# Norms between dense phases: the last feature tile and the first scaled tile in halves of 256 tokens, and the last but one tile's squares added on GpSimd

## What is computed

```python
def rms_norm(t, eps=NORM_EPS):
    tf = t.astype(jnp.float32)
    return (tf * lax.rsqrt(jnp.mean(tf * tf, axis=-1, keepdims=True) + eps)).astype(t.dtype)
...
        h = modulate(rms_norm(x), sh1, sc1)
        x = x + 0.5 * g1[:, None, :] * swiglu(h, w_ff1_in[l], w_ff1_out[l])
        h = modulate(rms_norm(x), sh2, sc2)
        z = h @ w_in[l]
...
        x = x + g2[:, None, :] * mixed
        h = modulate(rms_norm(x), sh3, sc3)
        x = x + 0.5 * g3[:, None, :] * swiglu(h, w_ff2_in[l], w_ff2_out[l])
```

## Time and profile before

| | us |
|---|---|
| median of 3 runs | 3761.18 |
| lowest and highest of them | 3758.82, 3763.38 |
| the profiled execution's own time | 3753.36 |
| its span, first to last instruction | 3751.6 |
| TensorE busy in that span | 3540.1 |
| VectorE, ScalarE, GpSimd busy | 1805.4, 1199.0, 626.3 |
| mean granted TensorE clock | 0.98 |

### The profile page before, as it was taken

One profiled execution on the slowest core, in us unless ns is written; L12 is line 12 of the kernel. 1 busy time (PEld: TensorE's weight loads), 2 busy tenths in 40 slices (PEclk: granted clock), 3 DMA queues, 4 the chain that ended last, 5 costly groups with the idle time before them and its releaser, 6 DMA issues. The chain is left out here.

```text
span 3751.6 us, 52300 instructions
## 1 busy us (share of the span) xinstructions
PE 3540.1 (94%) x22236; PEld 2797.3 (75%) x22236; DVE 1805.4 (48%) x2534; ACT 1199.0 (32%) x1659; POOL 626.3 (17%) x428
## 2 busy tenths in 40 slices
PE   7999998988999999999899899999799999989999
PEld 6888773686888788877458688867578887767887
DVE  5666536745544466653574533334543334354332
ACT  3222234523222322233352322233532223343223
POOL 4202002220202020210213020200011210001112
PEclk9999999999999999999999999999999999999999
DMA  6565421002443355532100233222123222122231
GB/s 193 172 200 162 130 69 34 7 26 80 135 152 110 121 160 179 161 126 72 34 7 13 93 90 107 81 74 79 46 79 101 94 87 93 46 68 85 95 101 57
DMA packets 445212, 358.01 MB, mean 95 GB/s; under 512 B 15990, under 2 KB 441012, under 8 KB 444980
## 3 DMA queue, kind: packets, MB, share of 16 engines
q1 hardware_dynamic: 444980, 354.67, 30.1%
HBM read 350.43 MB, written 2.10 MB: 94 GB/s over the span
## 5 line engine op out<-in xcount | busy, mean ns | idle before, releaser
L570 DVE TENSOR_TENSOR ring_wlo<-ring_raw,ring_whi 128x2048 fp32r<-128x2048 f32 (+4 forms) x270 | 576.6, 2136 | 407.6 <-ACT ring_whi L551 375.2
L551 ACT ACTIVATE ring_whi<-ring_raw 128x2048 fp32r<-128x2048 f32 (+3 forms) x278 | 491.1, 1767 | 533.6 <-PE f_ps L860 255.6
L858 PE MATMUL f_ps<-act_hi,ring_whi 128*128 128x512 f32 x1280 | 502.5, 393 | 3.3 <-DVEq L989 3.3
L860 PE MATMUL f_ps<-act_hi,ring_wlo 128*128 128x512 f32 x1280 | 498.6, 390 | 0.0
L859 PE MATMUL f_ps<-act_lo,ring_whi 128*128 128x512 f32 x1280 | 498.1, 389 | 0.0
L948 POOL TENSOR_TENSOR f_glo<-f_v,f_ghi 128x512 fp32r<-128x512 f32 x88 | 237.4, 2698 | 1082.2 <-ACT f_ghi L940 1082.2
L858 PEld LDWEIGHTS f_ps<-act_hi,ring_whi 128*128 128x128 f32 x1280 | 240.4, 188 | 53.8 <-DVEq L989 5.0
L933 ACT ACTIVATE f_t<-f_ps 128x512 f32<-128x512 f32 x88 | 52.6, 598 | 709.2 <-PE f_ps L860 656.3
L860 PEld LDWEIGHTS f_ps<-act_hi,ring_wlo 128*128 128x128 f32 x1280 | 240.2, 188 | 51.2
L858 PE MATMUL f_ps<-f_ghi,ring_whi 128*128 128x512 f32 x704 | 277.4, 394 | 0.0
L859 PEld LDWEIGHTS f_ps<-act_lo,ring_whi 128*128 128x128 f32 x1280 | 240.4, 188 | 48.9
(11 more groups left out here) (515 smaller groups left out, 6110.1 us busy)
## 6 DMA issues: line engine op xcount, KB each, us to landing
ring_raw<-in_w_ff_in SPq DMA_DIRECT2D x176, 512.0 KB, 4.8
f_ada_raw<-in_w_ada SPq DMA_DIRECT2D x128, 512.0 KB, 5.5
ring_raw<-in_w_mlp SPq DMA_DIRECT2D x64, 1024.0 KB, 5.2
ring_raw<-in_w_in SPq DMA_DIRECT2D x42, 1024.0 KB, 5.1
ring_raw<-in_w_ff_out SPq DMA_DIRECT2D x32, 768.0 KB, 4.8
ring_raw<-in_w_ff_out SPq DMA_DIRECT2D x32, 640.0 KB, 4.2
ring_raw<-in_w_out SPq DMA_DIRECT2D x16, 1024.0 KB, 5.2
ada_raw<-in_w_ada SPq DMA_DIRECT2D x16, 512.0 KB, 7.5
```

The costliest lines, as they stand in the source:

```text
L551: eng.activation(self.w_hi[:, i % self.SPLIT, 0:s.nk, 0:w], self.raw[:, i % self.RAW, 0:s.nk, 0:w], ACT.Copy)\
L570: eng.tensor_tensor(self.w_lo[:, i % self.SPLIT, 0:s.nk, 0:w], self.raw[:, i % self.RAW, 0:s.nk, 0:w], self.w_hi[:, i % self.SPLIT, 0:s.nk ...
L858: eng.matmul(out, wh, o_hi[:, a, :], start=(s.first and q == 0), stop=False)
L860: mm = eng.matmul(out, wl, o_hi[:, a, :], start=False, stop=(s.last and q == s.nk - 1))
```

## The change

The last slot before a norm makes its first output tile whole before its second, and signals that (`first_done`). VectorE updates x tile 6 on this signal, and tile 7 in two halves of 256 tokens. GpSimd adds tile 6's squares as well. ScalarE squares tile 7 in halves. TensorE sums each half of the tokens in a bank of its own (the second is one of the phase's own banks), four passes for the sum of GpSimd and four for tile 7, each of 256 columns. ScalarE takes Ln and Exp of the first half, then of the second. In `Norm`, tile 0 is scaled, rounded and subtracted in halves, and VectorE finishes its low part before it scales tiles 1 and 2. The diff, cut to its core:

```diff
+HALVES = (slice(0, S // 2), slice(S // 2, S))
...
 class Norm:
...
+    def steps(self, t):
+
+        return [(HALVES[0], 1), (HALVES[1], 2)] if t == 0 else [(slice(0, S), t + 2)]
+
     def scale(self, eng, t):
-        eng.scalar_tensor_tensor(out=self.part(t), in0=self.k.x[:, t, :], scalar=self.gain[:, t:t + 1], in1=self.k.rstd,
-                                 op0=ALU.mult, op1=ALU.mult).then_inc(self.scaled, 1)
+        for c, n in self.steps(t):
+            eng.scalar_tensor_tensor(out=self.part(t)[:, c], in0=self.k.x[:, t, c], scalar=self.gain[:, t:t + 1],
+                                     in1=self.k.rstd[:, c], op0=ALU.mult, op1=ALU.mult).then_inc(self.scaled, 1)
...
 class Sums:
...
+    def store(self, eng, wait_group, g, s, update):
+
+        if s.index < DT - 2:
+            wait_group(eng, g)
+            for m in (s.index, s.index + 1):
+                update(m, slice(0, S)).then_inc(self.x_done, 1)
+            eng.wait_ge(self.x_done, s.index + 2)
+        else:
+            eng.wait_ge(self.first_done, 1)
+            update(s.index, slice(0, S)).then_inc(self.x_done, 1)
+            wait_group(eng, g)
+            for c in HALVES:
+                update(s.index + 1, c).then_inc(self.x_done, 1)
+            eng.wait_ge(self.x_done, s.index + 3)
 
     def square(self, eng, t):
-        eng.wait_ge(self.x_done, t + 1)
         if t >= 2:
             eng.wait_ge(self.added, max(1, t - 2))
-        eng.activation(self.sq[t % 2], self.k.x[:, t, :], ACT.Square).then_inc(self.squared, 1)
+        for i, c in enumerate(HALVES if t == DT - 1 else [slice(0, S)]):
+            eng.wait_ge(self.x_done, t + 1 + i)
+            eng.activation(self.sq[t % 2][:, c], self.k.x[:, t, c], ACT.Square).then_inc(self.squared, 1)
 
     def add(self, eng, t):
-        if t == 0 or t >= DT - 2:
+        if t == 0 or t == DT - 1:
             return
...
-    def sum(self, eng):
-        eng.wait_ge(self.added, DT - 3)
-        eng.matmul(self.ps[:, :], self.k.ones, self.acc, start=True, stop=False)
-        for t in (DT - 2, DT - 1):
-            eng.wait_ge(self.squared, t + 1)
-            mm = eng.matmul(self.ps[:, :], self.k.ones, self.sq[t % 2], start=False, stop=(t == DT - 1))
-        mm.then_inc(self.summed, 1)
+    def sum(self, eng, banks_free, other_free):
+        eng.wait_ge(self.added, DT - 2)
+        eng.wait_ge(banks_free, other_free)
+        for c, ps in zip(HALVES, self.ps):
+            eng.matmul(ps[:, c], self.k.ones, self.acc[:, c], start=True, stop=False)
+        for i, (c, ps) in enumerate(zip(HALVES, self.ps)):
+            eng.wait_ge(self.squared, DT + i)
+            eng.matmul(ps[:, c], self.k.ones, self.sq[1][:, c], start=False, stop=True).then_inc(self.summed, 1)
 
     def invert(self, eng):
-        eng.wait_ge(self.summed, 1)
-        eng.activation(self.k.rstd, self.ps[:, :], ACT.Ln, scale=1.0 / D, bias=self.k.eps[:, 0:1]).then_inc(self.logged, 1)
-        eng.wait_ge(self.logged, 1)
-        eng.activation(self.k.rstd, self.k.rstd, ACT.Exp, scale=-0.5)
+        for i, (c, ps) in enumerate(zip(HALVES, self.ps)):
+            eng.wait_ge(self.summed, i + 1)
+            eng.activation(self.k.rstd[:, c], ps[:, c], ACT.Ln, scale=1.0 / D, bias=self.k.eps[:, 0:1]).then_inc(self.logged, 1)
+            eng.wait_ge(self.logged, i + 1)
+            eng.activation(self.k.rstd[:, c], self.k.rstd[:, c], ACT.Exp, scale=-0.5)
...
                 norm.scale(eng, 0)
+                norm.take_lo(eng, 0)
                 norm.scale(eng, 1)
-                for t in range(DT):
+                norm.scale(eng, 2)
+                for t in range(1, DT):
                     if t + 2 < DT:
                         norm.scale(eng, t + 2)
                     norm.take_lo(eng, t)
...
                 for q in range(DT):
-                    eng.wait_ge(norm.lo_ready, q + 1)
+                    eng.wait_ge(norm.lo_ready, q + 2)
...
+                if sums and i == n - 1:
+                    for q in range(s.nk):
+                        mm = block_of(q, 0)
+                    mm.then_inc(sums.first_done, 1)
+                    for q in range(s.nk):
+                        mm = block_of(q, 1)
```

More of the change, by code:

```diff
@@ L590, in round_hi @@
     def round_hi(self, eng, t):
[L591 to L607 removed]
+        for c, n in self.steps(t):
+            eng.wait_ge(self.scaled, n)
+            if self.shift is None:
+                ins = eng.activation(self.hi[:, t, c], self.part(t)[:, c], ACT.Copy)
+            else:
+                ins = eng.activation(self.hi[:, t, c], self.part(t)[:, c], ACT.Identity, bias=self.shift[:, t:t + 1])
+            ins.then_inc(self.hi_ready, 1)
@@ new lines, in take_lo @@
+    def take_lo(self, eng, t):
+        for c, n in self.steps(t):
+            eng.wait_ge(self.scaled, n)
+            eng.wait_ge(self.hi_ready, n)
+            part, hi = self.part(t)[:, c], self.hi[:, t, c].bitcast(F32)
+            if self.shift is None:
+                ins = eng.tensor_tensor(self.lo[:, t, c], part, hi, ALU.subtract)
+            else:
+                ins = eng.scalar_tensor_tensor(out=self.lo[:, t, c], in0=part, scalar=self.shift[:, t:t + 1], in1=hi,
+                                               op0=ALU.add, op1=ALU.subtract)
+            ins.then_inc(self.lo_ready, 1)
@@ L710, in products @@
         if sums:
-            sums = Sums(nc, k, ctx, name, rest, *room)
+            sums = Sums(nc, k, ctx, name, rest, ps[len(groups) % 2][0], *room)
         n_pairs = side.pairs if side else 0
@@ L849, in _, with block_of @@
                 o_hi, o_lo = operands[s.rhs]
-                for q in range(s.nk):
-                    a = s.k0 + q
-                    need(eng, own, base, s, q)
-                    if kind is Plain and g == 0:
-                        eng.wait_ge(norm.lo_ready, a + 1)
-                    for b, (c, w) in enumerate(s.tiles):
-                        out = ps[g % 2][b][0:w, :]
-                        wh, wl = ring.w_hi[:, at, q, c:c + w], ring.w_lo[:, at, q, c:c + w]
-                        eng.matmul(out, wh, o_hi[:, a, :], start=(s.first and q == 0), stop=False)
-                        eng.matmul(out, wh, o_lo[:, a, :], start=False, stop=False)
-                        mm = eng.matmul(out, wl, o_hi[:, a, :], start=False, stop=(s.last and q == s.nk - 1))
+                def block_of(q, b):
+                    c, w = s.tiles[b]
+                    a, out = s.k0 + q, ps[g % 2][b][0:w, :]
+                    wh, wl = ring.w_hi[:, at, q, c:c + w], ring.w_lo[:, at, q, c:c + w]
+                    eng.matmul(out, wh, o_hi[:, a, :], start=(s.first and q == 0), stop=False)
+                    eng.matmul(out, wh, o_lo[:, a, :], start=False, stop=False)
+                    return eng.matmul(out, wl, o_hi[:, a, :], start=False, stop=(s.last and q == s.nk - 1))
+                if sums and i == n - 1:
[4 more added lines that the diff above has]
+                        mm = block_of(q, 1)
+                else:
+                    for q in range(s.nk):
+                        need(eng, own, base, s, q)
+                        if kind is Plain and g == 0:
+                            eng.wait_ge(norm.lo_ready, s.k0 + q + 1)
+                        for b in range(len(s.tiles)):
+                            mm = block_of(q, b)
                 mm.then_inc(ring.slot_done, 1)
@@ L866, in _ @@
             if sums:
-                sums.sum(eng)
+                sums.sum(eng, banks_free, len(groups) - 1)
 def weights(w, l, col, width, k0, nk):
```

62 lines of the change are left out of this document (19 added, 43 removed).

## The result

| | before | after |
|---|---|---|
| median, us (lowest to highest, executions) | 3760.0 (3753.63 to 3763.38, 4) | 3732.21 (3730.37 to 3737.76, 4) |
| after over before | 1 | 0.9929 [0.9913, 0.9945] |
| the profiled execution, us | 3753.36 | 3732.57 |
| its span, us | 3751.6 | 3730.9 |

The changed kernel is faster by 0.71%. Its median lies 9.6 us under the forecast of 3741.8 and 2.8 us under the low end of the range.

What follows compares the result with a forecast made beforehand. TensorE bounds the kernel, waiting on a handover chain at 10 norm places. Gains of 9.35, 6.12, 1.21 + 1.20 and 0.66 + 0.84 sum to 19.4 us off 3761.18: 3741.8 us, 8-in-10 range 3735 to 3749.

Steps and rivals of the forecast that it cites:

- Bounds and places: TensorE bounds the kernel, and waits at 10 places where a dense phase's updated x needs its RMS norm: 8.06 or 7.93 us.
- Tile 6 leaves the chain: Before each norm: tile 6 is complete 4.1 or 5.5 us early; GpSimd's add costs nothing, slack 1.2 to 1.9 us.
- the two new waits: VectorE waits for the last slot's first half, TensorE for the second bank; both cost nothing.
- Halves: Halves cost more than half; sum of squares to rstd gains 1.21 or 1.20 us, rstd to restart 0.66 or 0.84.
- The first phases' 0.66 and 0.84: First f1 and first in2 gain only the rstd-to-restart part: 0.66 and 0.84 us.
- Tile 1 next: After the restart tile 1 comes 2.7 us after low 0, while TensorE has 12 passes on tile 0; no stall booked.
- Clock: Half clock after restarts, cold stretches of 3.2 to 5.7 us: no gain or loss booked, about 2 us of scatter.
- rival 3: GpSimd's tile 6 add is late in part, taking up to 3.33 us: gain 15, time 3746; 7%.
- Halves that don't pay (3765): Each half costs as much as its whole; places lose 0.3 to 0.5 us, no measurable change; 5%.
- The clock that stays up (3720): A restart 1.9 us sooner finds TensorE's clock still up; if no place went cold, 22 us saved; 5%.
- A late tile 6 (3746): GpSimd's tile 6 add ends 2.0 us later, past the slack in four places by 0.9 us; 7%.
- its slower form (3772): The late add stands before all eight passes in TensorE's queue, 3 us a place, slower than before; 3%.

Runs made afterwards that it cites:

- sums part alone: Kernel before with only tile 6 early and added on GpSimd, and tile 7's squares, sums, Ln and Exp in halves; norm unchanged: 3747.22 us, 0.9976 of before.
- tile 0 whole: Changed kernel with the norm's tile 0 whole again, its low part still ahead of scaling tiles 1 and 2: 3741.86 us, 0.9959 of before.

## Why the prediction was wrong, point by point

**Bounds and places: right.** The time went where the ten places are; the rest of the dense stages needs as many matmuls as before. The statement that a length change of the dense stages would speak against the prediction was fair too: the five dense stretches are 2.6 us shorter in sum, which is the half clock behind their restarts.

**Tile 6 leaves the chain: right.** The add was forecast to end at 437.8 in the kernel's old times and ended 1.01 us before the last dense matmul did (438.00, 439.01); forecast was 0.97 (438.77 - 437.8). GpSimd's add took 1283 to 1306 ns in all its 60 instances, as this one group shows:

```profile
L674 POOL TENSOR_TENSOR f_u<-f_u,f_v x20: 1285/1294/1299, 409.7 to 2491.6; 128x512 f32<-128x512 f32 x20
```

None took the 2.3 to 3.3 us of the slower operation in the earlier trace rows. Handing tile 6 back to TensorE costs 7.1 us. Reordered matmuls and the two new waits cost nothing that the timeline shows.

**Halves: right, the sizes within 0.2 us a place.** From the last matmul's end, forecast and measured:

| step | forecast | measured |
|---|---|---|
| sums of the first half begin | 1.03 | 1.08 |
| first Ln | 1.78 | 1.82 |
| first Exp | 2.29 | 2.32 |
| second Ln | 2.74 | 2.65 |
| second Exp ends | 3.67 | 3.56 |
| first scale | 3.96 | 3.84 |
| restart, with shift | 6.19 | 6.01 |
| restart, without shift | 5.89 | 5.79 |

The one term that was too large is ScalarE's: I put the second Ln behind the first Exp's end with 0.03 between, while it began 0.09 ahead of it (441.66, and 441.33 + 0.42). The Trainium skill's advice against small tiles ("VectorE: DVE Perf Modes", section "The TRN2 errata — SBUF-src ops pay a fixed extra latency per instruction") did not hold for this chain: tile 7 in halves is worth 11.8 us and tile 0 in halves 9.0. The bound taken for the passes of 256 columns (pitch halved, tail kept: 0.70) is what the row shows. A place gains 2.05 and 2.14 rather than 1.87 and 2.04; one place, mlp to in2, 2.44 (8.63 to 6.19 from the start of the last matmul). Over all places that is 20.4 us against 19.4.

**The first phases' 0.66 and 0.84: not seen for f1.** The first f1 restarts at 62.37 against 62.43. In the other profiles of the same two kernels it is 60.9, and 62.3 and 60.9, so the 0.66 is neither shown nor refuted.

**Tile 1 next: right.** No wait of TensorE stands between tile 0's matmuls and tile 1's. VectorE was busy for all of the 8 us behind each restart (8.00 in the rows above), and TensorE did not wait for it.

**Clock: this step failed.** It said: "I book no gain and no loss, and keep the spread", with the reason that the idle piece shrinks by only half a us (it shrank from 4.57 to 3.80), and it priced the stretches as draws from 3.2 to 5.7 us that average out over ten restarts. Behind eight of the ten they are no draws. They came out the same in every profile of the same program, 35.8 and 36.2 us before, 27.0, 25.9 and 26.1 after, and each edit of the chain set them anew, from 26 to 46 us. For the changed kernel they are 9 to 10 us less than before, 4.4 to 5 us of time where the sum has nothing. The low end of the range, 3735, left room for about 2 us of scatter and rival 3 above, and none for a gain of 5 on this side. That is the mistake: a term with a known size of about 18 us (35.8 / 2) before, whose change I could not work out, needed bounds on both sides in the range. The mixers' stretches, which the prediction doesn't mention, needed them too: between 1399 and 1411 us in the profiles without a fill, though no edit touched the mixers.

**The 9.6 us, as far as they can be told apart.** About 3 are the level: the forecast was set from a median of three of 3761.18, whereas 26 executions in one series gave 3758.03. One is the chain, 20.4 against 19.4. The other 5 to 6 are of the size of the half clock's 4.4 to 5, but it is not shown that they are that. The mixers' stretches took as much back in the profiles, and with the gaps filled in both kernels the medians still lie 25.8 us apart. So which stage gives the medians 4 us more than the chain stays open. From the profiled execution of the kernel before, the prediction had got 3734 by the same sum; those of the changed kernel took 3732.57, 3736.21 and 3730.68, 3733.2 in the mean. The forecast failed for the medians and held for the profiled executions.

**Why the stretches got shorter** is known only in outline. Shown: the whole stretch at half clock, the part ahead of the restart included, lasted 6.8 us in six of eight places before and 3.4 in seven of eight after (in all eight in the two other profiles), and with the sums part alone, where the half clock behind the restarts is longest, 6.8 in all eight; before, the clock had fallen ahead of the restart in every place, and in the changed kernel it was still up at the restart in four to six of the eight; delaying the restart by 1.05 us brings 35.8 us back. Argued: every dense stage is a fixed amount of work from one rise of the clock on, so its end, and with it the next restart, lies at a repeating distance from where the clock changes next, and a chain that is shorter by 2 us lands on another side of that change. What decides at which instant the clock falls was not isolated.

**The rivals.** Halves that don't pay (3765): refuted by the table above. The clock that stays up (3720): it does not, but it was half right; the time at half clock behind the eight restarts is shorter by a quarter. Its premise, that a sooner restart can find the clock still up, held in four to six of the eight places; its price, 22 us, came out well when it was made true by filling the gaps (19.4 and 20.5 us). The Trainium skill says in "TensorE: Matmul & The Clock Gate", section "HAM oscillation — how this bites in real kernels", that what helps is to avoid the idle gap; the runs with the filled gaps agree, while a gap of 6.4 rather than 8.5 us still went cold in all eight places. A late tile 6 (3746) and its slower form (3772): refuted, the add has a us to spare.

**Left open.** Both profiled executions of the kernel before (3753.36 and 3752.81) lie 5 us below its median of 3758, while the three of the changed kernel lie within 2 us of theirs; nothing here shows why. It makes the profiles' difference, 20.7 for the first pair and 19.9 in the mean, smaller than that of the medians, 24.

## What to carry to other kernels

Where TensorE waits for a chain of short handovers, halves pay even on engines that charge each instruction a fixed part, and work that can be done a little earlier on an idle engine should leave the chain; both can be summed from the rows to within 5%. Such a passage has a second price, the half clock behind its restart: read it (mean clock over a fixed stretch behind each restart, before and after), put its whole size into the range as long as its change is unknown, and don't take it for noise. Then look at the stages that were not touched as well, for they can take the gain back. Idle matmuls in the gap took it away for 20 us of 3733 here without lengthening the chain, but they must cover the longest gaps too.

## What the runs showed of the hardware

- The time at half clock behind the restarts that follow a dense stage directly repeats from execution to execution: 35.8 and 36.2 us over eight restarts in two profiles of one kernel, 25.9 to 27.0 in three of the other. Behind the renormalising phase it does not (0, 5.4 and 5.3 us). A shift of the restart by 0.34 us was enough to add 7 us of it (tile 0 whole).
- A shorter wait does not always mean less half clock: the sums part alone shortened the gaps by 1.32 us and lengthened the time at half clock from 35.8 to 46.2 us.
- Ten idle matmuls of 256 columns, a pause of 0.45 us and seventeen more kept the clock at 1.00 over a gap of 6.3 us; the 17 alone did so in the eight plain places and not in the renormalising phase.
- Five dense stretches took 1798.0 us with no half clock behind their restarts, 1805.6 with 16.0 us of it and 1808.4 with 21.9: it costs about half of itself. The four stretches with mixers in them took 1399 to 1411 us in profiles of kernels without a fill, though no edit touched the mixers.
- ScalarE begins an independent operation 0.33 us after the last began, though each shows 0.42 us at 256 columns: two squares took 0.75 together. Where the second waits for the first (Ln, Exp), they stand 0.49 to 0.50 apart.
